# Bisection steps placed between the head norm's products, one PSUM bank for the turned scores, and the meta tokens' rows moved behind them

## The reference, cut to what matters

```python
def attn_project(x, g, w_in, q_norm, k_norm, kidx_norm):
    ...
    q = rms_norm(q.reshape(B, L, N_HEADS, HEAD_DIM), q_norm)      # per head
    k = rms_norm(k.reshape(B, L, N_KV_HEADS, HEAD_DIM), k_norm)

def dsa_prompt(q, k, v, qi, ki, wi, topk):        # 128 of the keys per query
    ...
    sc = indexer_scores(qib, wib, ki, pos[None], k_pos)
    _, idx = lax.top_k(sc, topk)
    ...
    return sparse_attend(qb, k_sel, v_sel, idx <= pos[None, :, None])

def dsa_sample(q, k_new, v_new, qi, ki_new, wi, cache_k, cache_v, cache_kidx, page_table, topk):
    ...
    sc = indexer_scores(qi, wi, ki_all, q_pos[None], k_pos)
    _, idx = lax.top_k(sc, topk)                  # 256 of 2049 keys
    ...
    return sparse_attend(q, select(cache_k, k_new), select(cache_v, v_new), idx <= q_pos[None, :, None])
```

## Time and profile before

| | |
|---|---|
| Median of three runs | 2657.9 us (2656.54 to 2661.39) |
| Profiled execution, own time | 2655.82 us |
| Its span in the trace | 2654.0 us |
| PE busy | 94% of the span |
| DVE busy | 49% |
| ACT busy | 28% |
| POOL busy | 30% |
| Mean granted TensorE clock | 0.946 of full speed |

### The profile page before, as it was taken

How to read it: one execution, slowest core, us unless ns; L and a number is a source line. 1 busy time by engine, 2 the same in 40 slices (tenths; PEclk the granted TensorE clock), 3 DMA queues, 4 the chain that set the end, 5 groups by cost and what they waited for, 6 DMA issues and landing times.

```text
span 2654.0 us, 48017 instructions
## 1 busy us (share of the span) xinstructions
PE 2483.8 (94%) x19652; PEld 2334.6 (88%) x19652; DVE 1302.9 (49%) x1776; ACT 746.3 (28%) x1100; POOL 783.8 (30%) x467
## 2 busy tenths in 40 slices
PE   8999999996699999999999999999979639999999
PEld 8999999753467999999999999999968339999999
DVE  5333355766753533334533334677568742533333
ACT  4121232221243222212322222334566221322122
POOL 3311341242002433034432034202643343331130
PEclk9999999995589999999999999999989659999999
DMA  4223223244022222222222222423440002222312
GB/s 154 103 84 120 78 100 110 96 143 161 1 107 101 80 95 75 99 95 69 105 82 84 103 79 72 144 87 119 182 176 2 32 14 97 80 91 83 108 70 93
DMA packets 61002, 250.55 MB, mean 94 GB/s; under 512 B 9376, under 2 KB 25888, under 8 KB 41056
## 3 DMA queue, kind: packets, MB, share of 16 engines
q1 hardware_dynamic: 56672, 223.94, 23.9%
q0 software_dynamic: 4224, 25.17, 2.7%
HBM read 233.58 MB, written 15.49 MB: 94 GB/s over the span
## 4 chain that ended last, share of the span: by engine, by line
PE 87%; POOL 4%; DVE 4%; issue 3%; ACT 2%; DMA 0%; DVEq 0%; POOLq 0%; ACTq 0%
PE acc L598 46%; PE acc L628 22%; PE acc L753 4%; PE acc L1063 1%; PE acc L1999 1%; PE acc L911 1%; PE acc L1084 1%; POOL xT L2419 1%; PE acc L821 1%; PE acc L2046 1%; PE acc L1072 1%; PE acc L1052 1%; PE acc L2039 1%; POOL wl L2410 1%; POOL yl L2494 1%
## 5 line engine op out<-in xcount | busy, mean ns | idle before, releaser
L598 PE MATMUL acc<-xh,wh 128*128 128x268 f32 (+1 forms) x3344 | 685.1, 286 | 20.0 <-DVE xl L410 16.2
L598 PE MATMUL acc<-xl,wh 128*128 128x268 f32 (+1 forms) x3344 | 685.2, 286 | 0.0
L598 PE MATMUL acc<-xh,wl 128*128 128x268 f32 (+1 forms) x3344 | 682.8, 285 | 0.0
L598 PEld LDWEIGHTS acc<-xh,wh 128*128 128x128 f32 x3344 | 520.6, 189 | 21.0 <-issue 16.0
L401 DVE TENSOR_TENSOR wl<-raw,wh 128x2048 fp32r<-128x2048 f32 x185 | 430.6, 2328 | 205.7 <-ACT wh L342 205.7
L598 PEld LDWEIGHTS acc<-xh,wl 128*128 128x128 f32 x3344 | 521.6, 189 | 0.0
L598 PEld LDWEIGHTS acc<-xl,wh 128*128 128x128 f32 x3344 | 520.8, 189 | 0.0
L342 ACT ACTIVATE wh<-raw 128x2048 fp32r<-128x2048 f32 x194 | 370.3, 1909 | 506.2 <-PE acc L628 410.5
L553 POOL TENSOR_TENSOR gh<-scr,ones 128x536 f32 (+1 forms) x88 | 94.5, 1074 | 949.3 <-DVE scr L430 949.3
L423 DVE TENSOR_TENSOR scr<-acc,rstd 128x536 f32<-128x536 f32 (+1 forms) x88 | 62.7, 712 | 514.7 <-PE acc L598 514.6
L628 PE MATMUL acc<-gh,wh 128*128 128x268 f32 (+1 forms) x1408 | 287.7, 286 | 0.9 <-POOL gl L554 0.9
(11 more groups left out here) (423 smaller groups left out, 2992.9 us busy)
## 6 DMA issues: line engine op xcount, KB each, us to landing
raw<-in_w_ffn_in SPq DMA_DIRECT2D x88, 1024.0 KB, 4.8
raw<-in_w_ffn_out SPq DMA_DIRECT2D x32, 768.0 KB, 4.1
raw<-in_w_ssd_in SPq DMA_DIRECT2D x21, 1024.0 KB, 4.7
raw<-in_w_ffn_out SPq DMA_DIRECT2D x32, 640.0 KB, 3.8
raw<-in_w_attn_in SPq DMA_DIRECT2D x9, 1024.0 KB, 4.8
kic<-in_kpages SPq DMA_DIRECT2D x64, 128.0 KB
xT<-in_state_ssm SPq DMA_DIRECT2D x8, 1024.0 KB, 6.8
out_hs<-xT SPq DMA_DIRECT2D x8, 1024.0 KB, 5.0
```

The costliest lines, as they stand in the source:

```text
L598: mm = nc.tensor.matmul(acc[:, slot * 4 + 2 * t + h, 0:(N - lo) // 2], w[:, slot, c:c + P], x[:, kt, half_of(lo, h)], start=(kt == 0 and w ...
```

## The change: what it does

- **DVE.** The first `ask` and `last_round` come before the reciprocal of the head norm; answer 0, ask 1 and round 1 follow the reciprocal; after each of the ten multiplies come one `answer`, one `ask` and one `last_round`; `answer(11)` ends the row. The copy `q0s`, the masks of the query tiles (`picked`) and the meta rows' part on DVE come after that, and `picked(3)` after the meta rows' scores.
- **PE.** `turn_scores(0)` moves behind the head sums; turns 1 and 2 and `count(0)` follow it. A `count` stands behind each spread. Raw scores of sequence 4 stand ahead of spread 2 (before: spread 4), turn 3 and raw 5 ahead of spread 5 (before: turn 3 ahead of spread 4, raw 5 ahead of spread 8), turn 4 and raw 6 ahead of spread 8 (before: between counts 2 to 4, with the raw scores ahead of count 5). Turn 5, raw 7 and the own scores follow the meta rows' first products, turns 6 and 7 stand between the meta rows' later ones.
- **ACT.** The copies of the turned scores come behind the root, in one row from 0 to 4; 5, 6 and 7 stand between the meta rows' parts.
- **Bank.** All turned scores use bank 6, so each turn waits for the copy of the turn before; bank 7 is the counts' alone. Turn 0 now waits for `v_copied`.

Work is neither added nor left out: the same instructions run in another order.

```diff
@@ turn_scores
             if s:
                 pe.wait_ge(sscore_copied, s)
-            if s == 2:
+            else:
                 pe.wait_ge(v_copied, 3)
-            bank = 7 if s < 2 else 6
             for j in range(4):
-                mm = nc.tensor.transpose(acc[:, bank, j * P:(j + 1) * P], sraw[:, s % 2, j * P:(j + 1) * P], ident[:])
+                mm = nc.tensor.transpose(acc[:, 6, j * P:(j + 1) * P], sraw[:, s % 2, j * P:(j + 1) * P], ident[:])
@@ pe_attention
-        turn_scores(0)
         for n, t in enumerate(NORMED):
...
+        turn_scores(0)
+        turn_scores(1)
+        count(0)
+        turn_scores(2)
         pe.wait_ge(att_made, 1)
-        turn_scores(1)
-        turn_scores(2)
         pe.wait_ge(headread, 1)
         pe.wait_ge(sraw_ready, 4)
         for n in SPREADS:
-            if n == 4:
-                turn_scores(3)
+            if n == 2:
                 pe_raw_scores(pe, 4)
-            if n == 8:
-                pe_raw_scores(pe, 5)
+            if n in (5, 8):
+                turn_scores(3 + n // 8)
+                pe_raw_scores(pe, 5 + n // 8)
             if n >= 2:
                 pe.wait_ge(headread, n)
...
             mm.then_inc(headspread, 1)
+            count(n + 1)
+        count(len(SPREADS) + 1)
...
         mm.then_inc(first_asked, 1)
-        count(0)
+        turn_scores(5)
+        pe_raw_scores(pe, 7)
+        own_scores()
         pe.wait_ge(first_ready, 3)
...
         mm.then_inc(first_asked, 1)
-        count(1)
+        turn_scores(6)
         pe.wait_ge(first_ready, 4)
...
         mm.then_inc(first_asked, 1)
-        count(2)
+        turn_scores(7)
         pe.wait_ge(first_ready, 5)
-        for n in range(3, BEFORE):
-            if n == 3:
-                turn_scores(4)
-            if n == 5:
-                pe_raw_scores(pe, 6)
-            if n == 7:
-                turn_scores(5)
-            if n == 10:
-                pe_raw_scores(pe, 7)
-                own_scores()
-            count(n)
-        turn_scores(6)
-        turn_scores(7)
@@ act_attention
-            if n == 5:
-                turned_copy(0)
-                act_raw_copy(act, 2)
...
-        for s in range(1, 4):
+        for s in range(5):
             turned_copy(s)
             act_raw_copy(act, s + 2)
...
+        turned_copy(5)
+        act_raw_copy(act, 7)
         act.wait_ge(first_asked, 2)
...
+        turned_copy(6)
         act.wait_ge(first_asked, 3)
...
-        for s in range(4, S):
-            turned_copy(s)
-            if s + 2 < S:
-                act_raw_copy(act, s + 2)
+        turned_copy(7)
@@ dve_attention
+        dve.wait_ge(sdots_read, 1)
+        chain.link(nc.vector.memset(cand[:], 2.0 ** 15))
         dve.wait_ge(v_turned, 1)
...
         chain.link(nc.vector.tensor_copy(bias[:, 3], score_row(4)))
+        ask(0)
+        last_round(0)
...
         nc.vector.reciprocal(rstd[0:HROWS], rstd[0:HROWS]).then_inc(headread, 1)
+        answer(0)
+        ask(1)
+        last_round(1)
         for n in SPREADS:
...
+            answer(n + 1)
+            if n + 2 < BEFORE:
+                ask(n + 2)
+                last_round(n + 2)
+        answer(BEFORE - 1)
...
-        for j in range(1, 4):
-            picked(j)
-        dve.wait_ge(sdots_read, 1)
-        chain.link(nc.vector.memset(cand[:], 2.0 ** 15))
+        picked(1)
+        picked(2)
...
                                 ).then_inc(first_ready, 1)
...
-        for n in range(BEFORE):
-            ask(n)
-            if n == 1:
-                dve.wait_ge(first_done, 1)
-                chain.link(nc.vector.tensor_reduce(sum0[:], neg0[:], AX.X, ALU.add))
-                chain.link(nc.vector.reciprocal(sum0[:], sum0[:]))
-                nc.vector.tensor_tensor(neg0[:], neg0[:], sum0[:].unsqueeze(2).broadcast_to([P, 2, META]), ALU.mult
-                                        ).then_inc(first_ready, 2)
-            last_round(n)
-            answer(n)
-
+        picked(3)
+        dve.wait_ge(first_done, 1)
+        chain.link(nc.vector.tensor_reduce(sum0[:], neg0[:], AX.X, ALU.add))
+        chain.link(nc.vector.reciprocal(sum0[:], sum0[:]))
+        nc.vector.tensor_tensor(neg0[:], neg0[:], sum0[:].unsqueeze(2).broadcast_to([P, 2, META]), ALU.mult
+                                ).then_inc(first_ready, 2)
```

More of the change, by code:

```diff
@@ L960, in pe_attention, with count @@
             mm.then_inc(headsum, 1)
+        def count(n):
+            pe.wait_ge(count_asked, n + 1)
+            nc.tensor.matmul(acc[:, 7, 0:S], ones_b[:], cnt_b[:], start=True, stop=True).then_inc(count_done, 1)
+        turn_scores(0)
+        turn_scores(1)
+        count(0)
+        turn_scores(2)
         pe.wait_ge(att_made, 1)
-        turn_scores(1)
-        turn_scores(2)
         pe.wait_ge(headread, 1)
@@ L1236, in turned_copy @@
             nc.scalar.copy(Ss[:, s, 0:NPG, :].rearrange("p (q j) h -> p q j h", q=4),
-                           acc[:, 7 if s < 2 else 6, :].rearrange("p (j q h) -> p q j h", q=4, h=32)[:, :, :, 0:NH]
+                           acc[:, 6, :].rearrange("p (j q h) -> p q j h", q=4, h=32)[:, :, :, 0:NH]
                            ).then_inc(sscore_copied, 1)
@@ L1536, in dve_attention @@
                               ).then_inc(dve_side, 1)
[L1537 to L1552, removed]
@@ L1563, in dve_attention @@
[L1563 to L1568, removed]
-        s0 = acc[:, 2, 0:2 * META].rearrange("p (a m) -> p a m", a=2)
-        chain.link(nc.vector.scalar_tensor_tensor(neg0[:], s0, -QSCALE, mask0[:].unsqueeze(1).broadcast_to([P, 2, META]),
-                                                  ALU.mult, ALU.subtract))
@@ L1572, in dve_attention @@
-        chain.link(nc.vector.tensor_reduce(min0[:], neg0[:], AX.X, ALU.min))
-        nc.vector.tensor_tensor(neg0[:], neg0[:], min0[:].unsqueeze(2).broadcast_to([P, 2, META]), ALU.subtract
-                                ).then_inc(first_ready, 1)
         def over_groups(ap):
@@ new lines, in dve_attention @@
+        chain.link(nc.vector.tensor_copy(bias[:, 3], score_row(4)))
+        ask(0)
+        last_round(0)
+        dve.wait_ge(headsq, len(NORMED) + 1)
+        nc.vector.reciprocal(rstd[0:HROWS], rstd[0:HROWS]).then_inc(headread, 1)
+        answer(0)
+        ask(1)
+        last_round(1)
+        for n in SPREADS:
+            dve.wait_ge(headspread, n + 1)
+            t = NORMED[n]
+            x = halves(hT[:, t])
+            nc.vector.scalar_tensor_tensor(x, x, headg[:, 1:2] if t >= K0 else headg[:, 0:1],
+                                           acc[:, (n % 2) * 2:(n % 2) * 2 + 2, 0:H], ALU.mult, ALU.mult).then_inc(headread, 1)
+            answer(n + 1)
+            if n + 2 < BEFORE:
+                ask(n + 2)
+                last_round(n + 2)
@@ new lines, in dve_attention @@
+        answer(BEFORE - 1)
+        dve.wait_ge(headread, len(SPREADS) + 1)
+        nc.vector.tensor_copy(q0s.rearrange("p (t m) -> p t m", m=META), hT[:, 0:QT, 0:META]).then_inc(att_made, 1)
+        picked(1)
+        picked(2)
+        dve.wait_ge(first_asked, 1)
+        nc.vector.tensor_copy(mask0[:], acc[:, 3, 0:META]).then_inc(dve_side, 1)
+        groups = acc[:, 3, 256:512].rearrange("p (a b d) -> p a b d", a=2, b=2)
+        inb = in_block[:].rearrange("p (r b) -> p r b", b=2)
+        for a in range(2):
+            ins = nc.vector.tensor_tensor(vpad[a], groups[:, a].unsqueeze(1).broadcast_to([P, REP, 2, HD]),
+                                          inb.unsqueeze(3).broadcast_to([P, REP, 2, HD]), ALU.mult)
+            ins.then_inc(att_made if a else dve_side, 1)
@@ new lines, in dve_attention @@
+        dve.wait_ge(att_made, 4)
+        s0 = acc[:, 2, 0:2 * META].rearrange("p (a m) -> p a m", a=2)
+        chain.link(nc.vector.scalar_tensor_tensor(neg0[:], s0, -QSCALE, mask0[:].unsqueeze(1).broadcast_to([P, 2, META]),
+                                                  ALU.mult, ALU.subtract))
+        chain.link(nc.vector.tensor_reduce(min0[:], neg0[:], AX.X, ALU.min))
+        nc.vector.tensor_tensor(neg0[:], neg0[:], min0[:].unsqueeze(2).broadcast_to([P, 2, META]), ALU.subtract
+                                ).then_inc(first_ready, 1)
```

14 lines of the change are left out of this document (6 added, 8 removed).

## The result

The changed kernel takes 2642.34 us (median of 5 runs, 2641.07 to 2644.14), the kernel before 2656.8 us on the same chip (5 runs, 2652.74 to 2661.39). The ratio is 0.9944, its 95% interval [0.9932, 0.9955]: 14.5 us less, by the interval 12 to 18. The forecast was 2647.6 us (2643 to 2653) and 10.3 us less. The profiled execution took 2641.9 us (span 2640.2, before 2654.0).

The account below looks back on a forecast made before the run. PE was taken to bound the stretch's first half and DVE the second; sweep 39.4 plus tail 11.2 us against 60.3, with 0.6 ahead, is 10.3 us less: 2657.9 - 10.3 = 2647.6 us, range 2643 to 2653.

Parts of the forecast that it names:

- The spreads are done ahead of DVE's round: Sweep: PE's ordinary spreads hidden with 2.5 us to spare; rival, each starting only after DVE's round, 2655 us, chance 0.06.
- The stalls: Sweep: DVE waits for PE at multiplies 2, 5 and 8, forecast 1.0, 1.35 and 1.35 us, 3.7 in all.
- The middle value: Stalls at spreads 5 and 8: 1.35 us each, taken between 2.0 at the low clock and 0.7 at the high.
- slower: Rival: the loop over pairs loses its high clock, up to 23 us more, 2671 us; chance 0.04.
- given back: Rival: the loop waits for something that didn't move, so the stretch's gain is lost, 2656 us; chance 0.05.
- Beside POOL's gathers: Sweep: the skill's page suggests contention with DVE's compares; the forecast added nothing, steps taking 2.47 and 2.48 us.
- The tail on PE: From DVE's last answer to the loop's first product: forecast 11.2 us, bounds 9.9 and 13.
- the six hand-overs: Tail on PE: 0.1 us added for each of six hand-overs, 0.6 us in the sum.
- The sweep: DVE's joined answers, asks, rounds and multiplies after the reciprocal: 35.7 us plus 3.7 of waits, 39.4 us.
- Ahead of the reciprocal: Turn 0 moved behind the head sums lets the sums start 0.6 us earlier.
- raw 6 or 7 wait for keys: Named sign of a wrong prediction: raw scores of sequence 6 or 7 waiting for key transfers; some 8 us allowed for landing.
- The clock rival: Rival: high clock granted through the sweep and the tail, 2644.1 us, the lower bound; chance 0.15.

Follow-up runs that it names:

- e11_steps_behind: Changed kernel with only the interleaving undone (ten spreads and multiplies first, then the steps): 2652.29 us in one execution, beside 2641.85 us of the changed kernel.
- e2_one_bank: Kernel before with only bank 6 for all turns, turn 0 behind the head sums, ACT's copies 0 to 3 behind the root: 2706.85 us, ratio 1.0015.
- e12_same: Changed kernel, no edit, on a chip where the kernel before takes 2655.4 us: 2641.85 us, ratio 0.9947 to the kernel before.
- the third group: Follow-up runs on a chip where the kernel before takes 2655.4 us; the changed kernel, unedited, took 2641.85 us there.
- e8_same_again: Changed kernel, no edit, on a chip where the kernel before takes 2706.0 us: 2686.48 us, ratio 0.9928 to the kernel before.
- e3_steps_behind: Changed kernel with only the interleaving undone, on a chip where the kernel before takes 2702.8 us: 2707.32 us, ratio 1.0008 to the kernel before.
- e5_before: The kernel before, unedited, one execution on a slower chip for its profile: 2699.42 us.
- e7_split_raws: Changed kernel with raws 4, 5 and 6 as two halves, each ahead of its own spread: 2689.49 us, ratio 0.9940 to the kernel before.
- e6_raw7_early: Changed kernel with turn 5 ahead of count 10, raw 7 behind it, turns 6 and 7 ahead of the meta rows' transposes: 2691.1 us, ratio 0.9944 to before.
- e1_same: Changed kernel, no edit, on a chip where the kernel before takes 2702.8 us: 2687.5 us, ratio 0.9947 to the kernel before.

## Why the prediction had the direction and not the size

**What held.** The mechanism is the one argued. PE's spare time and DVE's lay in different halves and now lie over each other: with the steps taken out of the sweep again, 12.3 of the 12.8 us up to the loop's first product are gone (e11_steps_behind). The turns in one bank alone bring no gain (e2_one_bank). The spreads are done ahead of DVE's round: seven of ten multiplies waited for nothing. The stalls came at multiplies 2, 5 and 8 with 0.92, 1.41 and 1.42 us, 3.75 in all, where 1.0, 1.35 and 1.35 were forecast. The middle value that I took for the last two stands for what the rows show, a turn at the low clock (1.08 us) and a spread at the high one (1.17). The first came out for another reason: spread 2 took 1.31 us and not 1.88, and the multiply started 0.47 us after its end by PE's rows, which nothing in them explains. In e12_same the three are 0.78, 1.43 and 2.41 us, so the close agreement is in part luck. The loop and all behind it only moved: neither of the rivals in the loop, slower or given back, came true. Beside POOL's gathers the compares take 0.30 us as before, but for one of 0.34 at 604.49 that starts together with a gather (604.50).

**What was mis-sized.** The stretch gave 15.2 us, the sum 10.3. By its own terms:

- *The tail on PE*, "11.2 us", with bounds of 9.9 and 13, is the term that failed: measured, from 632.01 to 640.96, it is 8.95 us, below the lower bound, and 8.95 us again in e12_same. Of the 2.27 us less than forecast, 0.6 are the six hand-overs, which cost nothing: between the q0s copy and the last turn PE's rows show no idle time. 1.24 are the clock, high from the end of raw 7 on: turn 6 took 0.61 us instead of 1.05, from turn 7 to the loop it was 1.33 instead of 1.78, the transposes took 0.39 instead of 0.59, and from the meta rows' last products to turn 7 it was 0.54 instead of 0.69. The rest, 0.43, is that I added durations: groups of products overlap at their ends (own scores have 0.96 us and the next work starts 0.89 after them).
- *The sweep*, "39.4 us", took 38.2 (593.83 to 632.01). The stalls were right in sum, the iteration was 3.16 us (599.34 less 596.18) and not 3.28: a multiply of 0.77 us is followed by the answer after 0.69, so I had added 0.03 us where 0.08 had to come off, ten times.
- *The loop's first products* had no term. They took 2.20 us instead of 3.81, 1.6 us less. In the other profiles of the changed kernel it is 0.1, 0.6 and 0.8 us less, so in this one most of it is luck.
- *Ahead of the reciprocal*, "0.6 us": 0.43.

The terms' errors, 2.3 + 1.2 + 1.6 - 0.2, are 4.9 us, the whole difference between 10.3 and 15.2 in this execution. The medians differ by 14.5. In e12_same, whose chip takes the same time, the stretch gave 13.4 us against the kernel before: the tail 2.3 us more than forecast, the sweep 0.4, the loop's first products 0.6. So the tail is the error that comes again.

One sign of being wrong that I had named, that raw 6 or 7 wait for keys, did not show on the chips of the first measurement and of the third group, but did on the two slower ones: raw 7 waited 1.69 and 2.50 us, and the tail took 11.1 and 12.0 us.

**The clock rival** was half right. Through the sweep the clock changed between its levels, 0.68 on average from 594 to 634, as the forecast took it. In the tail it was high from raw 7 on (in e8_same_again only from the meta rows' last products on). I had read in the earlier trace rows that raw scores are followed by 1.00, and had used that for the stalls, but not for the tail, in which raw 7 is followed by six short groups. The lower bound of 9.9 us took the turns at the high clock, and nothing else.

**What stays open.** Why the loop's first products find the high clock in one execution (2.20 us) and the low one in another (3.69) in the same order. Why the clock behind raw scores is high in most places and low in some. And, on the two slower chips alone, what DVE and ACT waited for where PE's rows had ended 2 to 9 us before: at the copy `vnew` in every profile of them, with 5 us, and behind raw 5 or 6 in e3_steps_behind, e5_before and e7_split_raws. That the keys' transfers hold up something there would fit the place, but no run tests it.

## What to carry to other kernels

- Where two strands on the same two engines have opposite limits, put the steps of one between the products of the other. Then look at what is left as PE's work against DVE's cover, for each iteration and for several in a row: raw scores and a spread take 5.0 us from the count on, and 5.9 with a turn, which is more than the cover of 4.8 and made the three stalls of the changed kernel. Three iterations in a row with some 4.1 us of PE each, against 3.16 of DVE, brought stalls too, though each alone is within the cover (e7_split_raws).
- In a sum over a pipelined engine use the time from one start to the next, and no hand-overs where the other side is early. Durations and hand-overs came out 0.11 us too high for each of ten multiplies and some 1.0 us in a tail of 9.
- Moving work that reads a transfer forward is worth nothing where the transfer isn't done; and where work queued behind it is on the critical path, its wait becomes theirs (e6_raw7_early, 8.82 us). How early a transfer is done can differ by chip.

## What the runs showed of the hardware

- What stands before a piece of work goes with its clock, but doesn't fix it. In four profiles of the changed kernel the spread behind the sixteen 128x512 products of raw 4, 5 or 6 took 1.17 to 1.31 us in nine places, 1.58 and 1.71 us in two, and 2.15 us in one. Behind eight of these products it took 2.15 us in four places of six. And a busy engine doesn't always have the high clock: the kernel before stayed at 0.50 for 11.8 us in which PE was never idle, with spreads of 20 rows, a turn and raw scores.
- The raw scores themselves took 3.64 us at a granted clock of 0.50 (598.0 to 601.6 in the first profile) and 3.64 us at 0.61 (609.5 to 613.0).
- On two chips the kernel before takes 2703 and 2706 us, on the others 2655 and 2657. Raw 7's keys there are late by 1.7 to 2.5 us in the changed order, and on the others not at all. SP's queue is busy with its sixteen transfers of keys for 25.7 and 26.6 us there (e1_same, e8_same_again), and for 19.8 and 19.7 us on the others.
- On the two slower chips the kernels with the steps behind spread over 10 us (2700 to 2710), the changed kernel over 2 to 3 (2687.15 to 2689.03, 2685.18 to 2687.71). The interleaved order has also taken away most of that spread; why is open.
